# ada_w's shift and scale columns loaded and summed in two halves, and another order of the query tiles in attention

## What is computed

```
mod = silu(c) @ ada_w + ada_b                      # c (1024), ada_w (1024, 3072)
shift, scale, gate = split(mod, 3)
h = rmsnorm(x, norm_g) * (1 + scale) + shift
z = h @ w_in                                       # 2760 columns: xr gr q k v ga qi ki wi
y_r = rg_lru(conv(xr)) * silu(gr)                  # recurrence, 512 channels
score = sum over 8 index heads of relu(qi.ki / 8) * wi / sqrt(8), causal
idx = top 256 of score for each query
y_a = softmax(q.k / 8 over idx) @ v * silu(ga)     # 8 heads of 64, one shared key and value
x = x + gate * (concat(y_r, y_a) @ w_out)
out = rmsnorm(x, final_g)
```

## Time and profile before

| | us |
|---|---|
| median of 3 runs | 621.33 |
| lowest and highest of them | 620.89, 621.44 |
| the profiled execution | 619.93 |
| its span, from first to last instruction | 618.1 |

### The profile page before, as it was taken

The page is one execution under the profiler, slowest core; times in us unless marked ns, Lnnn a source line. Parts: engine busy times, 40 slices in busy tenths (PEclk is TensorE's granted clock), DMA queues, the critical chain, the costliest instruction groups (busy, mean ns, idle before and its releaser), DMA issues.

```text
span 618.1 us, 8029 instructions
## 1 busy us (share of the span) xinstructions
PE 535.4 (87%) x2676; PEld 444.8 (72%) x2676; DVE 439.5 (71%) x992; ACT 377.4 (61%) x679; POOL 233.5 (38%) x195
## 2 busy tenths in 40 slices
PE   1459989998999999999999526489999999999994
PEld 1346868777787777778888415478889999888873
DVE  5987386885999889898697886854475666664522
ACT  6513236453499999987898555554466666656531
POOL 5150862352344274677642003740402030313322
PEclk9859999998999999999999855569999999999999
DMA  8967342430112111135550420110011000101011
GB/s 335 418 206 266 105 118 53 102 85 18 36 34 69 34 36 34 35 103 137 140 133 0 177 96 0 68 36 2 8 61 43 28 36 34 41 30 69 0 69 68
DMA packets 16457, 51.96 MB, mean 84 GB/s; under 512 B 4000, under 2 KB 5024, under 8 KB 15392
## 3 DMA queue, kind: packets, MB, share of 16 engines
q1 hardware_dynamic: 16416, 51.45, 26.3%
HBM read 37.81 MB, written 4.19 MB: 68 GB/s over the span
## 4 chain that ended last, share of the span: by engine, by line
PE 68%; DVE 11%; DMA 7%; POOL 5%; ACT 4%; issue 3%; SPq 2%; DVEq 0%; POOLq 0%; ACTq 0%
PE pair L1373 30%; PE pair L1470 13%; PE pair L1492 6%; PE pair L1505 5%; DMA ada<-in_ada_w 4%; PE pair L1448 3%; PE pair L1449 2%; DMA qs<-half_lo 2%; PE pair L1422 2%; DVE rank L1156 2%; PE pair L1514 2%; PE pair L1413 2%; PE pair L1414 2%; DVE tie L1158 1%; POOL half_lo L726 1%
## 5 line engine op out<-in xcount | busy, mean ns | idle before, releaser
L1373 PE MATMUL pair<-h_hi,w_hi 128*128 128x512 f32 (+1 forms) x352 | 114.4, 407 | 1.6 <-DVE h_lo L1064 1.5
L1373 PE MATMUL pair<-h_lo,w_hi 128*128 128x512 f32 (+1 forms) x352 | 109.8, 393 | 0.0
L1373 PE MATMUL pair<-h_hi,w_lo 128*128 128x512 f32 (+1 forms) x352 | 109.0, 391 | 0.0
L1298 DVE TENSOR_TENSOR pt_lo<-pair,pt_hi 128x512 fp32r<-128x512 f32 (+3 forms) x96 | 50.5, 554 | 71.1 <-ACT pt_hi L963 70.5
L858 ACT ACTIVATE bias_sb<-score_sb,tinies 128x1024 bf16<-128x1024 f32 (+2 forms) x93 | 95.7, 1032 | 3.2 <-DVE tinies L1109 3.1
L696 POOL TENSOR_SCALAR w_hi<-w_raw 128x1024 fp32r<-128x1024 f32 (+1 forms) x22 | 29.4, 1339 | 136.3 <-PE pair L1373 120.5
L1373 PEld LDWEIGHTS pair<-h_hi,w_hi 128*128 128x128 f32 (+1 forms) x352 | 65.0, 188 | 19.0 <-issue 6.2
L1373 PEld LDWEIGHTS pair<-h_lo,w_hi 128*128 128x128 f32 (+1 forms) x352 | 66.0, 188 | 15.5 <-issue 0.8
L1373 PEld LDWEIGHTS pair<-h_hi,w_lo 128*128 128x128 f32 (+1 forms) x352 | 65.6, 186 | 15.4 <-issue 0.7
L1095 DVE TENSOR_SCALAR_CACHE_REDUCE bias_sb<-score_sb,tinies 128x640 bf16<-128x640 f32 (+2 forms) x93 | 72.6, 802 | 0.9
L781 POOL TENSOR_TENSOR x_res<-q_free,x_res 128x512 f32<-128x512 f32 x14 | 18.1, 1296 | 121.0 <-DVE q_free L1269 121.0
(11 more groups left out here) (195 smaller groups left out, 1254.2 us busy)
## 6 DMA issues: line engine op xcount, KB each, us to landing
w_raw<-in_w_tiles SPq DMA_DIRECT2D x21, 512.0 KB, 3.5
ada<-in_ada_w SPq DMA_DIRECT2D x8, 1024.0 KB, 18.4
x_sb<-in_x SPq DMA_DIRECT2D x8, 512.0 KB, 7.1
ada_g<-in_ada_w SPq DMA_DIRECT2D x8, 512.0 KB, 4.5
qs<-half_hi SPq DMA_DIRECT2D x16, 256.0 KB, 3.6
qs<-half_lo SPq DMA_DIRECT2D x16, 256.0 KB, 4.4
wo_raw<-in_w_out SPq DMA_DIRECT2D x8, 512.0 KB, 6.4
x_res<-in_x SPq DMA_DIRECT2D x8, 512.0 KB, 3.3
```

The lines of the kernel that those rows point to most:

```text
L1298: nc.vector.tensor_tensor(pt_lo[:, 4 * b:4 * b + nc4, hh, :], psum[use % 2][:, 0:nc4 * P].rearrange("p (c q) -> p c q", q=P), f32(pt_hi[:, ...
L1373: ins = nc.tensor.matmul(psum[banks[half]][0:width, :], w[b][:, k, 0:width], hh[:, k, half * HALF:(half + 1) * HALF], start=(k == 0 and p ...
```

## The change

Shift's and scale's columns are cut into two halves of four blocks of 128 channels each, and each `ada` tile becomes two tiles of [128, 2, 512], 512 KB each, in runs of 2 KB. SP loads slab 0, the eight first halves, slab 1, the eight second halves. DVE sums the first half of all eight row tiles, then two tiles of the second, then finishes `mod` for the first half (`modulation(0)`), two more sums, then `h_lo[k]` and a sum in turn for four k, then `modulation(1)` and the last four `h_lo[k]`. The step `xt = xt * scale + shift` moves from DVE to ACT, which makes `h_hi[k]` from the unscaled `xt` and then rewrites `xt[k]` with the same operation. PE adds up the first half, runs `kstep(0, k)` and `kstep(1, k)` in turn from k = 0, and adds up the second half ahead of k = 3. `FIRST_US` becomes 37, and `ATT` takes tiles 3 and 2 ahead of 7, 6 and 5.

```diff
-MOD_GROUPS = [(0, 3), (3, KC)]
+MOD_GROUPS = [(0, KC // 2), (KC // 2, KC)]
...
-ATT = [1, 0, 4, 7, 6, 5, 3, 2]
+ATT = [1, 0, 4, 3, 2, 7, 6, 5]
...
-FIRST_US = 46.0
+FIRST_US = 37.0
...
-        ada = [sb(f"ada{k}", R_H + 8192 * k, [P, 2048]) for k in range(KC)]
+        ada = [[sb(f"ada{k}_{n}", R_H + 32768 * (k // 4) + 16384 * n + 4096 * (k % 4), [P, 2, D // 2]) for n in range(2)] for k in range(KC)]
...
-        acc_ok = sem("acc_ok")
+        acc_ok = [sem(f"acc_ok{n}") for n in range(2)]
+        mod_ok = sem("mod_ok")
...
-            for k in range(KC):
-                sp.dma_start(ada[k][:, :], ada_w[k * P:(k + 1) * P, 0:2 * D]).then_inc(ada_in[k], 16)
-                if k >= KC - 2:
-                    load_slab(k - (KC - 2))
+            for n in range(2):
+                load_slab(n)
+                for k in range(KC):
+                    src = ada_w[k * P:(k + 1) * P, 0:2 * D].rearrange("p (b m) -> p b m", b=2)
+                    sp.dma_start(ada[k][n][:, :, :], src[:, :, n * (D // 2):(n + 1) * (D // 2)]).then_inc(ada_in[k][n], 16)
...
             for k in range(KC):
-                act.wait_ge(h_full, k + 1)
-                nc.scalar.activation(h_hi[:, k, :], xt[:, k, :], ACT.Copy).then_inc(h_hi_ok, 1)
+                act.wait_ge(mod_ok, k // (KC // 2) + 1)
+                act.wait_ge(xt_act, 2 * KC)
+                shift, scale = mod[:, k:k + 1], mod[:, 8 + k:9 + k]
+                nc.scalar.activation(h_hi[:, k, :], xt[:, k, :], ACT.Identity, bias=shift, scale=scale).then_inc(h_hi_ok, 1)
+                act.wait_ge(h_hi_ok, k + 1)
+                nc.scalar.activation(xt[:, k, :], xt[:, k, :], ACT.Identity, bias=shift, scale=scale).then_inc(h_full, 1)
...
+            def accumulate(k, n):
+                g0, g1 = MOD_GROUPS[n]
+                v_acc = acc[:, :].rearrange("p (b m) -> p b m", b=2)[:, :, g0 * P:g1 * P]
+                dve.wait_ge(ada_in[k][n], 16)
+                if k == 0:
+                    dve.wait_ge(c_ok, 1)
+                    nc.vector.tensor_scalar(v_acc, ada[k][n][:, :, :], c_act[:, k:k + 1], None, ALU.mult).then_inc(acc_ok[n], 1)
+                else:
+                    dve.wait_ge(acc_ok[n], k)
+                    nc.vector.scalar_tensor_tensor(v_acc, ada[k][n][:, :, :], c_act[:, k:k + 1], v_acc, ALU.mult, ALU.add).then_inc(acc_ok[n], 1)
+            def modulation(n):
+                g0, g1 = MOD_GROUPS[n]
+                dve.wait_ge(mod_ps, n + 1)
+                v_mod, v_ps, v_b = (t.rearrange("p (b k) -> p b k", b=2)[:, :, g0:g1] for t in (mod[:, :], psum[7 - n][:, 0:16], sm[:, 16:32]))
+                link(nc.vector.tensor_tensor(v_mod, v_ps, v_b, ALU.add))
+                nc.vector.scalar_tensor_tensor(mod[:, 8 + g0:8 + g1], mod[:, 8 + g0:8 + g1], 1.0, sm[:, 8 + g0:8 + g1], ALU.add, ALU.mult).then_inc(mod_ok, 1)
+            def low_half(k):
+                dve.wait_ge(h_full, k + 1)
+                nc.vector.tensor_tensor(h_lo[:, k, :], xt[:, k, :], f32(h_hi[:, k, :]), ALU.subtract).then_inc(h_lo_ok, 1)
             for k in range(KC):
-                dve.wait_ge(ada_in[k], 16)
-                for n, (g0, g1) in enumerate(MOD_GROUPS):
-
-                    v_acc, v_ada = (t[:, :].rearrange("p (b m) -> p b m", b=2)[:, :, g0 * P:g1 * P] for t in (acc, ada[k]))
-                    if k == 0:
-                        dve.wait_ge(c_ok, 1)
-                        nc.vector.tensor_scalar(v_acc, v_ada, c_act[:, k:k + 1], None, ALU.mult).then_inc(acc_ok, 1)
-                    else:
-                        dve.wait_ge(acc_ok, len(MOD_GROUPS) * (k - 1) + n + 1)
-                        nc.vector.scalar_tensor_tensor(v_acc, v_ada, c_act[:, k:k + 1], v_acc, ALU.mult, ALU.add).then_inc(acc_ok, 1)
-
-            dve.wait_ge(xt_act, 2 * KC)
-            for k in range(KC):
-                for n, (g0, g1) in enumerate(MOD_GROUPS):
-                    if k == g0:
-                        dve.wait_ge(mod_ps, n + 1)
-                        v_mod, v_ps, v_b = (t.rearrange("p (b k) -> p b k", b=2)[:, :, g0:g1] for t in (mod[:, :], psum[7 - n][:, 0:16], sm[:, 16:32]))
-                        link(nc.vector.tensor_tensor(v_mod, v_ps, v_b, ALU.add))
-                        link(nc.vector.scalar_tensor_tensor(mod[:, 8 + g0:8 + g1], mod[:, 8 + g0:8 + g1], 1.0, sm[:, 8 + g0:8 + g1], ALU.add, ALU.mult))
-                nc.vector.tensor_scalar(xt[:, k, :], xt[:, k, :], mod[:, 8 + k:9 + k], mod[:, k:k + 1], ALU.mult, ALU.add).then_inc(h_full, 1)
-                if k:
-                    dve.wait_ge(h_hi_ok, k)
-                    nc.vector.tensor_tensor(h_lo[:, k - 1, :], xt[:, k - 1, :], f32(h_hi[:, k - 1, :]), ALU.subtract).then_inc(h_lo_ok, 1)
-            dve.wait_ge(h_hi_ok, KC)
-            nc.vector.tensor_tensor(h_lo[:, KC - 1, :], xt[:, KC - 1, :], f32(h_hi[:, KC - 1, :]), ALU.subtract).then_inc(h_lo_ok, 1)
+                accumulate(k, 0)
+            accumulate(0, 1)
+            accumulate(1, 1)
+            modulation(0)
+            accumulate(2, 1)
+            accumulate(3, 1)
+            for k in range(KC // 2):
+                low_half(k)
+                accumulate(KC // 2 + k, 1)
+            modulation(1)
+            for k in range(KC // 2, KC):
+                low_half(k)
...
-            for g, (g0, g1) in enumerate(MOD_GROUPS):
-                pe.wait_ge(acc_ok, len(MOD_GROUPS) * (KC - 1) + g + 1)
+            def mod_sums(g):
+                g0, g1 = MOD_GROUPS[g]
+                pe.wait_ge(acc_ok[g], KC)
                 for n in [*range(g0, g1), *range(KC + g0, KC + g1)]:
                     ins = nc.tensor.matmul(psum[7 - g][:, n:n + 1], acc[:, n * P:(n + 1) * P], ones[:, :], start=True, stop=True)
...
+            mod_sums(0)
             for k in range(KC):
-                kstep(0, k)
-                if k >= KC // 2:
-                    kstep(1, k - KC // 2)
-            for k in range(KC // 2, KC):
-                kstep(1, k)
+                if k == KC // 2 - 1:
+                    mod_sums(1)
+                for j in range(2):
+                    kstep(j, k)
             for o in ORDER["PE"]:
                 if o[0] == "kstep" and o[1] >= 2:
                     kstep(o[1], o[2])
```

More of the change, by code:

```diff
@@ L479, in layer_kernel @@
         x_in = [sem(f"x_in{t}") for t in range(NT)]
-        ada_in = [sem(f"ada_in{k}") for k in range(KC)]
+        ada_in = [[sem(f"ada_in{k}_{n}") for n in range(2)] for k in range(KC)]
         w_in_s = [sem(f"w_in{b}") for b in range(2)]
```

## The result

The changed kernel takes 625.59 us as the median of four runs (623.34 to 626.54), beside 621.11 for the kernel before. The ratio is 1.0081, with a 95% interval from 1.0066 to 1.0095: 5.0 us slower, 4.1 to 5.9. Forecast were +3.7 us and 625.0.

A forecast was written before the change was run, and what follows sets the result against it. PE's work was taken as the bound, with the queries' stacking through POOL and a DMA beside it in the head. Later first score 1.9, clock 1.8, tile order 0: +3.7 us on 621.33, so 625.0; range 617.5 to 628.5.

The forecast's parts named there:

- the main step of the head: Tiles 0 and 1: tile 0 ends at 63.4, tile 1 at 64.8; POOL's split of slab 2 waits for tile 0.
- PE's new wait: Behind tile 1, ahead of kstep(2, 0): PE waits 2.7 us for POOL's split of slab 2.
- The planner's order: Whole kernel: the planned order of operations should stay the same, costed at nothing, within 1 us either way.
- The sum: Whole kernel: 1.9 us later first score, 1.8 for the clock, 0 for the tile order, +3.7 us in all.
- The first kstep: Head: PE's first kstep starts at 37.4 instead of 45.14, 7.7 us earlier.
- The clock in k = 0: First ksteps of tiles 0 and 1: the twelve matmuls of k = 0 at half clock, 5.1 us.
- Slab 3's split: POOL's queue ahead of the index scores: the split takes 6.0 us beside DVE's gate products, 4.1 at the least.
- The clock: At the first index score: PE idles 6.6 us, then runs 3.7 us at half speed, 1.8 us lost.
- ATT: Attention and output: the new tile order only moves PE's idle time, 0 in sum, from -0.8 to +1.2 us.
- The early start: Rival for the head: a quicker POOL queue carries the early start on, gain 2.4 us, 618.9; chance 0.22.
- The lock: Rival: POOL's splits block DVE's first sums fully, 5.7 us instead of 1.4, time 629; chance 0.08.
- part 1: The forecast's stretch of the head until PE's first kstep, put at 37.4 us.

The follow-up runs named there:

- slabs23_early: Changed kernel with slab 2 split into its own buffer after the second half's sums, slab 3 into slab 0's buffer once tile 0 ends; 620.72 us.
- slabs23_warm: slabs23_early plus unused matmuls in PE's waits: 8 ahead of the first index score, 13 ahead of head 6, 5 ahead of v's transposes; 619.07 us.
- warm_after: Changed kernel plus unused matmuls in PE's waits: 10 ahead of tile 2, 18 and 13 ahead of index scores, 5 ahead of v's transposes; 620.61 us.
- tile0_first: Changed kernel with PE running the last two ksteps of tile 0 ahead of the last two of tile 1; 625.15 us.
- slab2_early: Changed kernel with slab 2 split into a buffer of its own right behind slab 1, no longer waiting for tile 0; 624.19 us.
- warm_tile2: Changed kernel plus 10 unused matmuls ahead of tile 2 alone; 625.71 us.
- the filled kernels: Changed kernel and kernel before, each with unused matmuls in PE's waits; 620.61 us and 618.22 us.
- the head's alone: Changed kernel with the old order of query tiles, so only the head is changed; 624.9 us, ratio 1.0047.

## Why the prediction was right, and where not

**Right, the main step of the head.** "Tile 1 gains 4.7 us, tile 0 loses 0.7, and POOL hangs on tile 0." Tile 1 ended at 65.9 instead of 69.5 (3.6 gained), tile 0 at 64.4 instead of 62.7 (1.7 lost). PE's new wait was 2.47 us (2.7 forecast), the wait ahead of k = 4 1.53 (1.3), the second sums 1.84 (1.75). The first score moved by +0.8 us (+1.9). The experiments confirm the mechanism by taking it away: slabs23_early brings the scores 3.2 us earlier, and slabs23_warm against warm_after shows that the time follows. The planner's order, put at no cost, is the same: `stages()` gives identical lists for every engine in both kernels.

**The sum, right in part by luck.** Forecast were 1.9 us for the later first score, 1.8 for the clock behind it, 0 for the order. The profile has 0.8 at the first score, no fall of the clock behind it (full from 85.9 to 92), 0.8 in small pieces up to the transposes of v, 1.3 behind them where the clock fell, and 0.6 for the order. Neither term of the sum was right by itself; too much at and behind the scores stood against small pieces, a fall at 272 and an order of tiles that the sum had at nothing. That 625.59 lies 0.6 us from the forecast is no measure of the working.

**The first kstep, 37.4 forecast, 38.90 measured.** Two terms were short, and one sum was off: from 33.6 two operations of 1.06 us end at 35.7, not at 35.9. DVE's eight sums took 11.95 us, from 18.85 to 30.80, where I had 11.3, and DVE came to them 0.6 us later. ACT's operations took 1.24 us each where I took 1.06 from the plain copy; for each k that is 2.41 us, not 2.2. ScalarE: Activation LUTs, a page of the Trainium skill, says under "What ACT_TABLE_LOAD costs" that each [128,1] pointer operand adds about 93 ns to an ACTIVATE; two of them, 0.19 us, fit the 1.24 against 1.06. The prediction left them out.

**The clock in k = 0.** I took 5.1 us at half speed; it rose 2.7 us after the first kstep, and 1.2 us of the late start came back. The two misses nearly cancel, which is luck: in slabs23_warm the clock rose 4.7 us after it.

**Slab 3's split.** I took 6.0 us because DVE's gate products would lie beside it. It took 4.1, as before, 70.61 to 74.70: the clock had fallen in tile 2, wi came late, and so did DVE's products. Where the clock held in tile 2 and the products came earlier, the split took 4.9 us, in warm_after and in tile0_first, and the scores came at 86.81 and 85.64. So the direction was right and 6.0 was too much; with 4.9 the same sum would have put the first score at 86.0.

**The clock, right in kind, wrong in place and size.** I expected the clock to hold over 2.5 us of waiting, since it had at 82.7, and to fall behind 6.6 us ahead of the scores, for 1.8 us. It fell behind the 2.47 us already, in tile 2, which took 3.4 us longer for it, and so PE's wait ahead of the scores was 1.20 us and the clock held there. Where PE did wait about 5 us for the scores (5.09 in tile0_first, 5.20 in slab2_early, 5.10 in warm_tile2), the clock fell behind it. The fall in tile 2 was hidden (warm_tile2). The clock's price lies elsewhere: it fell at 272 as well, and the waits near 142 and 272 may or may not cost the clock in a given run.

**The parts, from the filled kernels.** The changed kernel loses 4.3 us by the clock and the one before 2.5, so the change adds 1.8, give or take 1.4 by the intervals (that 1.8 was forecast too is a coincidence: the forecast had it in one fall behind the first score); the filled kernels differ by 0.51%, 3.2 us give or take 1.1 (2.4 by their medians), of which the scores' later start is 1.5 (86.81 against 85.34) and the order of tiles 0.6 to 1.4, so by the ratios 0.3 to 1.1 has no place of its own. The two filled profiles differ by 2.2 us, near the medians' 2.4, and place it all: 1.5 at the first score, 1.6 at the transposes of v, 1.7 at the third tile's output, 2.3 at the last pieces. In all 1.8 + 3.2 = 5.0.

**ATT.** Forecast 0, from -0.8 to +1.2; measured about 1. "A longer chain of tile 5 behind step 63" was the end that came true. The waits at tiles 3 and 2 moved with them, all but unchanged: 0.17 and 0.82 us, at 467.82 and 491.24, where they had been 0.15 and 0.82.

**The rivals.** The early start was not carried. The lock did not cost its full price in part 1: the sums took 0.7 us more than forecast and not 4.3. From 41.6 to 47.4 us in slab2_early, DVE's three operations beside POOL's split took 6.6 us instead of 3.7, so DVE lost about half of the time that the two ran side by side, not whole instructions as this rival had it; POOL lost as well, 5.8 us for a split that takes 3.6 alone.

**Open.** The changed kernel's profiled execution was quicker by 2.2 us than its median. That typical runs spend more time at half clock is on record by their mean clocks; where the further falls lie was not seen. Why the same wait lowers the clock in one execution and not in another stays open too.

## What to carry to other kernels

Before you start a stage earlier, follow the queue of each engine behind it: here 6.2 us of head start ended at a POOL queue that hung on the one tile which the new order finished later. With the two tiles interleaved from the start, the first one ended 1.7 us later, and the split that needed its buffer lost its cover. Price a wait of TensorE by two terms, the wait and the clock behind it, and if the wait can't be removed, matmuls without use in it were cheap here: they gave 2.5 us (0.40%) on the kernel before.

## What the runs showed of the hardware that was not expected

- TensorE's clock fell behind a wait of 2.47 us in one place (66 to 68.3, then 0.56 until 76) and not behind one of 2.52 us in another. Behind the same wait of 3.2 us near 142 it fell in the changed kernel's profile and not in the head's alone. Each fall there cost 1.6 us. So no length of a wait by itself told here whether the clock would fall behind it.
- Runs of 2 KB instead of 8 KB in ada_w's loads cost little: 390 GB/s between 16 and 26 us, against 424 before; 387 against 394 between 26 and 34.
- An ACTIVATE of 1024 columns with a scale and a bias from memory takes 1.24 us, the copy 1.06.
- Beside POOL's splits, DVE's L1057 took up to 2.10 us for 1024 columns instead of 1.28, and L1054 1.75 instead of 1.28. The first L1054, at 18.85, lay beside POOL's split of slab 0 and took 1.28 all the same.
